# Softmax weights moved into a diagonal matrix product, a shorter pipeline, and another order in the delta-rule scan, in a three-block transformer kernel

## The reference, cut to what matters

```python
# first block: three branches per head, 8 heads of 64, gated and added
p_c = softmax(q @ k_cmp.T + bias)      # 31 compressed keys
p_s = softmax(q @ k_slc.T + bias)      # causal keys, selected blocks
p_w = softmax(q @ k_win.T + bias)      # causal keys, window
out = g0 * (p_c @ v_cmp) + g1 * (p_s @ v_slc) + g2 * (p_w @ v_win)

# third block: 768 keys (256 of context, 512 of the sequence)
o_diff = softmax(q1 @ k1.T) @ v - lam * softmax(q2 @ k2.T) @ v   # 4 heads
o_mla  = softmax(qn @ kn.T + qr @ kr.T) @ v                      # 4 heads

# second block, the gated delta rule, in 8 chunks of 64 tokens, 4 heads
new    = u[chunk] - w[chunk] @ state          # "fresh"
answer = q_dec[chunk] @ state + a_qk[chunk] @ new
state  = g_end * state + k_dec[chunk].T @ new
```

## Time and profile before

| | us |
|---|---|
| median of 3 runs (4128.83 to 4129.73) | 4129.71 |
| the profiled execution | 4129.73 |
| its span in the trace | 4127.9 |
| PE busy | 3511.0 (85%) |
| DVE busy | 2328.0 (56%) |
| ACT busy | 1536.9 (37%) |

### The profile page before, as it was taken

How to read it: one execution, slowest core, us unless ns; L and a number is a source line. 1 busy time by engine, 2 the same in 40 slices (tenths; PEclk the granted TensorE clock), 3 DMA queues, 4 the chain that set the end, 5 groups by cost and what they waited for, 6 DMA issues and landing times. The chain is left out here.

```text
span 4127.9 us, 45959 instructions
## 1 busy us (share of the span) xinstructions
PE 3511.0 (85%) x15671; PEld 2637.0 (64%) x15672; DVE 2328.0 (56%) x2916; ACT 1536.9 (37%) x1926; POOL 140.4 (3%) x124
## 2 busy tenths in 40 slices
PE   6778798999958688899879778775999999999996
PEld 4646687774446457688652645554777777777774
DVE  3355675338232245445440547435888888888885
ACT  1143332010023431110110215314777777777772
POOL 0000000000000100000000000002000000000001
PEclk8889999999979899699989889977999999999997
DMA  4311222222111100022216300116999999999995
GB/s 144 104 47 42 82 91 93 77 95 82 62 36 46 32 11 1 27 95 99 81 61 232 102 31 19 34 58 273 387 361 366 353 362 365 355 350 363 363 351 197
DMA packets 172315, 653.53 MB, mean 158 GB/s; under 512 B 14953, under 2 KB 82377, under 8 KB 114226
## 3 DMA queue, kind: packets, MB, share of 16 engines
q1 hardware_dynamic: 154370, 605.44, 40.2%
q0 software_dynamic: 7568, 25.70, 1.7%
q10 hardware_dynamic: 10272, 20.98, 1.3%
HBM read 610.98 MB, written 36.77 MB: 157 GB/s over the span
## 5 line engine op out<-in xcount | busy, mean ns | idle before, releaser
L378 DVE TENSOR_TENSOR experts_rest<-experts_weights,experts_leading 128x2048 fp32r<-128x2048 f32 x384 | 875.3, 2286 | 100.1 <-ACT experts_leading L2894 100.1
L2894 ACT CAST experts_leading<-experts_weights 128x2048 fp32r<-128x2048 f32 x384 | 715.4, 1904 | 46.9 <-ACT experts_y L2886 23.1
L384 PE MATMUL psum<-experts_leading,experts_xT_leading 128*128 128x512 f32 x1024 | 409.3, 400 | 51.6 <-DVE experts_rest L378 51.6
L385 PE MATMUL psum<-experts_rest,experts_xT_leading 128*128 128x512 f32 x1024 | 406.8, 397 | 0.0
L386 PE MATMUL psum<-experts_leading,experts_xT_rest 128*128 128x512 f32 x1024 | 402.5, 393 | 0.0
L384 PEld LDWEIGHTS psum<-experts_leading,experts_xT_leading 128*128 128x128 f32 x1024 | 194.6, 190 | 107.8 <-DVE experts_rest L378 65.4
L386 PEld LDWEIGHTS psum<-experts_leading,experts_xT_rest 128*128 128x128 f32 x1024 | 194.4, 190 | 44.6
L385 PEld LDWEIGHTS psum<-experts_rest,experts_xT_leading 128*128 128x128 f32 x1024 | 194.9, 190 | 40.2
L384 PE MATMUL psum<-experts_leading,experts_hidden_leading 128*128 128x512 f32 x512 | 210.3, 411 | 0.0
L386 PE MATMUL psum<-experts_leading,experts_hidden_rest 128*128 128x512 f32 x512 | 202.0, 394 | 0.0
L385 PE MATMUL psum<-experts_rest,experts_hidden_leading 128*128 128x512 f32 x512 | 200.9, 392 | 0.0
(11 more groups left out here) (664 smaller groups left out, 6923.2 us busy)
## 6 DMA issues: line engine op xcount, KB each, us to landing
experts_weights<-in_w_up SPq DMA_DIRECT2D x256, 1024.0 KB, 6.9
experts_weights<-in_w_down SPq DMA_DIRECT2D x128, 1024.0 KB, 6.8
merge_weights<-in_w_merge SPq DMA_DIRECT2D x32, 768.0 KB, 4.2
ada_weights<-in_w_ada SPq DMA_DIRECT2D x24, 1024.0 KB, 6.8
ff_up_weights<-in_w_up SPq DMA_DIRECT2D x22, 1024.0 KB, 4.8
expert_rows<-experts_y ACTq DMA_DIRECT2D x66, 256.0 KB, 7.2
down_weights<-in_w_down SPq DMA_DIRECT2D x16, 704.0 KB, 5.1
out_weights<-in_w_out SPq DMA_DIRECT2D x6, 1536.0 KB, 8.7
```

The costliest lines, as they stand in the source:

```text
L378: return dve.tensor_tensor(out, src, leading.bitcast(F32), ALU.subtract)
L384: pe.matmul(out, lh, rh, start=start, stop=False)
L385: pe.matmul(out, lh, rl, start=False, stop=False)
L2894: act.copy(leading[h % LEADING], place(ring, h)).then_inc(masked, 1)
```

## The change

In `paired_attention` the probabilities are no longer scaled. `weigh` writes a diagonal matrix per half (identity times factor, [128 x 2 x 128] in one DVE operation), and `turn` multiplies the raw probabilities with it, as a matrix product instead of a transpose. Where the pair is `joined`, the two halves are added in PSUM, so both are turned. LAG becomes 1 and 2 instead of 2 and 3, with the buffers one less deep, and `weigh(s)` is done in step s (wide) or `weigh(s - 1)` (narrow). In the scan, the state part of the answer moves from before the update to behind it, head by head, paired with the second part.

```diff
-    LAG, HELD = (2, 1) if wide else (3, 2)
+    LAG, HELD = (1, 1) if wide else (2, 2)
...
+        diag = sb("diag", [P, DEEP, 2, P])
...
-                    for h in hs if not joined else (0,):
+                    for h in hs:
                         for n, (lo, keys, _) in enumerate(u.tiles):
-                            last = pe.transpose(k.psum[0:keys, turned_at(h) + n * P:turned_at(h) + (n + 1) * P],
-                                                probs[:, b, h, lo:lo + keys], k.c("ident"))
+                            last = pe.matmul(k.psum[0:keys, turned_at(h) + n * P:turned_at(h) + (n + 1) * P],
+                                             probs[:, b, h, lo:lo + keys], diag[:, b, h, :],
+                                             start=(not joined or (h == 0 and n % (BANK // P) == 0)),
+                                             stop=(not joined or h == 1), skip_group_check=joined)
...
-                    if joined:
-                        dve.tensor_scalar(probs[:, b, 0, 0:u.keys], probs[:, b, 0, 0:u.keys], inverse[:, b, 0:1], None,
-                                          ALU.mult).then_inc(scaled, 1)
-                        dve.wait_ge(scaled, p + 1)
-                        dve.scalar_tensor_tensor(probs[:, b, 0, 0:u.keys], probs[:, b, 1, 0:u.keys], inverse[:, b, 1:2],
-                                                 probs[:, b, 0, 0:u.keys], ALU.mult, ALU.add).then_inc(weighed, 1)
-                    else:
-                        dve.tensor_tensor(probs[:, b, :, 0:u.keys], probs[:, b, :, 0:u.keys],
-                                          inverse[:, b, :].unsqueeze(2).broadcast_to([P, 2, u.keys]), ALU.mult
-                                          ).then_inc(weighed, 1)
+                    if p >= DEEP:
+                        dve.wait_ge(turned, per * (p - DEEP + 1))
+                    dve.tensor_tensor(diag[:, b, :, :], k.c("ident").unsqueeze(1).broadcast_to([P, 2, P]),
+                                      inverse[:, b, :].unsqueeze(2).broadcast_to([P, 2, P]), ALU.mult).then_inc(weighed, 1)
...
-                    v = step - (LAG - 1)
+                    v = step if wide else step - 1
```

In the scan:

```diff
-                    if n >= 2:
-                        pe.wait_ge(taken, n - 1)
-                    answer = k.psum[:, (2 + n % 2) * BANK:(2 + n % 2) * BANK + H * C].rearrange("p (h c) -> p h c", h=H)
-                    for h in range(H):
-                        pe.matmul(answer[:, h, :], state[:, n % 2, h, :], q_dec[:, h, tok], start=(h == 0), stop=False,
-                                  skip_group_check=True)
                     pe.wait_ge(corrected, n + 1)
...
                     last.then_inc(learned, 1)
+                    if n >= 2:
+                        pe.wait_ge(taken, n - 1)
                     for h in range(H):
                         hs = slice(h * P, (h + 1) * P)
-                        last = pe.matmul(answer[:, h, :], fresh[rows, n % 2, hs],
...
+                        o = k.psum[:, (2 + n % 2) * BANK + h * C:(2 + n % 2) * BANK + (h + 1) * C]
+                        pe.matmul(o, state[:, n % 2, h, :], q_dec[:, h, tok], start=True, stop=False)
+                        last = pe.matmul(o, fresh[rows, n % 2, hs], a_qk[rows, t, h * P + rows.start:h * P + rows.stop],
+                                         start=False, stop=True)
                     last.then_inc(answered, 1)
```

More of the change, by code:

```diff
@@ L864, in paired_attention @@
         top, total, inverse = (sb(x, [P, DEEP, 2]) for x in ("top", "total", "inverse"))
+        diag = sb("diag", [P, DEEP, 2, P])
         turned_sb = sb("turned", [P, 2, 2 * BANK])
-        scored, masked, exped, inverted, gated, scaled, weighed, turned, copied, summed, taken, passed = (sem(x) for x in (
-            "scores_ready", "scores_masked", "probs_ready", "sums_inverted", "inverses_gated", "probs_scaled", "weights_ready", "probs_turned",
+        scored, masked, exped, inverted, gated, weighed, turned, copied, summed, taken, passed = (sem(x) for x in (
+            "scores_ready", "scores_masked", "probs_ready", "sums_inverted", "inverses_gated", "weights_ready", "probs_turned",
             "probs_copied", "values_summed", "results_taken", "waits_passed"))
@@ L2125, in _ @@
                     last.then_inc(learned, 1)
+                    if n >= 2:
+                        pe.wait_ge(taken, n - 1)
                     for h in range(H):
                         hs = slice(h * P, (h + 1) * P)
-                        last = pe.matmul(answer[:, h, :], fresh[rows, n % 2, hs],
-                                         a_qk[rows, t, h * P + rows.start:h * P + rows.stop], start=False, stop=(h == H - 1),
-                                         skip_group_check=True)
+                        o = k.psum[:, (2 + n % 2) * BANK + h * C:(2 + n % 2) * BANK + (h + 1) * C]
+                        pe.matmul(o, state[:, n % 2, h, :], q_dec[:, h, tok], start=True, stop=False)
+                        last = pe.matmul(o, fresh[rows, n % 2, hs], a_qk[rows, t, h * P + rows.start:h * P + rows.stop],
+                                         start=False, stop=True)
                     last.then_inc(answered, 1)
```

## The result

| | before | after |
|---|---|---|
| median, us | 4129.72 | 4196.35 (4 runs, 4187.81 to 4198.76) |
| profiled execution, us | 4129.73 | 4197.81 |
| its span | 4127.9 | 4196.0 |
| PE / DVE / ACT busy | 3511.0 / 2328.0 / 1536.9 | 3581.7 / 2292.7 / 1538.5 |

The ratio after to before is 1.0163, 95% interval 1.0150 to 1.0175 (over all 21 executions of the changed kernel, 4187.81 to 4203.06): by the medians 66.6 us slower, where 52.9 were forecast. The time lies inside the range of 4165 to 4200, near its upper end.

What follows compares the result with a forecast made beforehand. PE was taken to bound all four stages, with DVE close in nsa and diff. Terms of 29.7 (diff), 10.5 (nsa), 5.9 (mla) and 6.8 (scan) gave +52.9 on 4129.73: 4182.6 us, range 4165 to 4200.

Steps and rivals of the forecast that it cites:

- The price of a product: Attention turns: 0.23 us per fp32 product, two records of 0.115 as in the fox stretch, against 0.11 to 0.13 per transpose.
- The rivals with cheap products: Attention turns: products cost as little as transposes (0.11; 4136 us; chance 0.04) or about 0.06 (4121 us; chance 0.03).
- the chain rival: diff and nsa: with the short lag the dependency loop binds, not PE; +8 us each, 4199 in all; chance 0.15.
- First turn hidden in the gap, second in the open: mla: first turn grows 0.74 into a wait of 0.94, second adds 0.74 per pair, x 8 = +5.9 us.
- with the low clock until 2484.6: diff: laid out from 2465.1 at the low clock until then, the stage ends at 2570.6 instead of 2540.9, +29.7 us.
- the clock rival: Heads of nsa and diff: denser PE work gets the high clock at once, realistically 8 us less, 4175; chance 0.08.
- the tiles: nsa: longer turns over 160 transposes of 128 keys and 32 of 31 keys add 4.6 us per head pair, 18.5 in all.
- the shorter lag: diff: its loop of 5.69 us stays under PE's 5.83 per pair; mla: 0, bound -2; no separate term in nsa.
- The 8 given back: nsa: of 4.6 us PE waiting per head pair 2.6 remain as DVE scaling shrinks; 2.0 returned each, 8 in all.
- The gap of 0.85: Scan: PE idles 0.85 us per chunk ahead of the update (L2114), waiting for DVE's `fresh`; x 8 = +6.8.
- The same 1.90 of L2118 comes later: Scan: the moved state part keeps its 1.90 us, so the chunk grows by 0.85 only.
- The "relief" of DVE: Less DVE scaling buys back 8 us in nsa and 0.23 x 16 = 3.7 in diff.

Runs made afterwards that it cites:

- The attentions alone: The changed `paired_attention` with the scan as in the kernel before; 4175.35 us, ratio 1.0104 to the kernel before.
- the products with the identity: The kernel before with each transpose replaced by an fp32 product with the identity, scaling and lag as before; 4156.09 us, ratio 1.0056.
- the diagonal with the old lag: The changed attentions with LAG 2 and 3 as before, and the old scan; 4172.51 us, ratio 1.0091 to the kernel before.
- the lag alone: The kernel before with only LAG 1 and 2, transposes and DVE scaling kept; 4171.48 us, ratio 1.0096.
- the blocks: The kernel before with the scan's state part behind the update as one block of four, not head by head; 4140.18 us, one run.
- the copy put first: The kernel before with ACT, in mla only, copying the second half ahead of the next exponential; 4118.90 us, ratio 0.9979.

## Why the prediction was right, and where it wasn't

**The price of a product: right.** 0.116 per record in diff and 0.121 with the identity, 0.115 priced from fox. The products' cost is all of mla and most of diff and nsa. The rivals with cheap products fall.

**The total: right in part by luck.** Measured less forecast, the four stages are off by +7.9 (nsa), +12.1 (scan), -7.2 (diff) and -0.2 (mla). The range reached up to 4200 for the sake of the chain rival, with its 8 us each in diff and nsa; half of that came in nsa, none in diff. What filled the range was mostly the scan's order, which no rival had.

**mla: right, step by step.** First turn hidden in the gap, second in the open, step 10.07 against 10.1.

**diff: the mechanism right, the size 7.2 too large.** The pair takes 5.70 to 5.71 instead of 5.83, PE bound, as said: 16 x 0.13 = 2.1. The other 5.1 is put down to the term "with the low clock until 2484.6", 19.5 into the stage: the full clock now came after 3.4 (1.00 over the attention, before: 0.87). The attentions alone bear this out: the same instructions at the low clock for 7.4 us more took 2.3 longer, which for 16 us makes 5.0, an estimate. That is the clock rival, at some 5 of its 8 us. Why it rose isn't settled. The kernel before and the five variants that leave diff as it was had it after 19.5 to 19.6; the products with the identity after 16, the attentions alone after 10.8, the diagonal with the old lag after 3.1 with a fall between 6.5 and 13.4. But the lag alone, whose turns are all transposes, had it after 9.3, and the attentions alone have the changed kernel's very instructions. The Trainium skill, page "TensorE: Matmul & The Clock Gate", Part 4, has it that transposes don't count as PE activity in the same way. The lag alone shows that this can't be the whole of it, since it rose 10 us earlier with the same transposes. No run here isolates that rule.

**nsa: wrong by 7.9.** Three steps failed. First, the tiles: turns of 4, 8, 12, 16 records take 0.64, 1.09, 1.54, 1.98, some 0.1 more than priced, and 31-key turns 0.55; by these the work grows by 23.4, not 18.5 (by the profile's busy time, from 93.0 to 115.8, by 22.8). I had laid fox's spacing end to end without the group's own edges. Inside a turn records start 0.112 apart, but the first stands up to 0.213 from the second, and the last 0.205 from the values, whose weights have another shape (`128*64` behind `128*128`). In diff, where the values have the turn's shape, that last one is 0.111. Second, "the shorter lag" was priced at nothing in nsa, and is worth 4.5 there. The chain rival had this ("with one step less of slack"), and was right in nsa on the cause, with half its size, though not in diff. Third, the waits given back were laid to DVE's smaller scaling; the two variants between show that this is worth 0.8 beside the longer turns, and that what goes back, goes because PE's longer turns cover the waits (they fall by 7.5 in the identity variant). The 8 given back came out right for the old lag for a wrong reason: PE's waits were 13.7 before, 5.3 with the diagonal and the old lag, 9.3 in the changed kernel. The account closes: 22.8 of work instead of 18.5 (+4.3) and 4.4 given back instead of 8 (+3.6) make 7.9.

**The scan: wrong by 12.1.** The gap of 0.85 is right to the hundredth. The step that failed is "The same 1.90 of L2118 comes later": it comes later and interleaved, and the order of two kinds of product was priced at nothing. Per chunk 0.85 for the gap; ten changes of the weights' shape instead of three, seven more at 0.19, make 1.33; and 0.11 is lost because the update no longer has the second part right behind it (there the next record started 0.107 later, half of the 0.213 inside a block). Together 2.29 for each of seven chunks. The first chunk, which begins at the full clock, grew by 8.79 - 5.91 = 2.88: 18.9 in all, as measured. Of this the blocks show 0.85 + 0.19 + 0.11 = 1.15, the interleaving the other 1.14.

The "relief" of DVE (35 us less to do) gives next to nothing back by itself: 0.8 in nsa, nothing in mla, and in diff the 0.23 of waiting per pair that the longer turns cover too. What it does in diff is to make the short lag bearable. In all four stages PE has the most work, and it took 70.7 more.

## What to carry to other kernels

A change that moves work from a busy engine to the busiest one is priced by the latter's records alone; what the former gains counts only where it still ends a wait after the first has grown. A term that says "the same instructions, only in another order" needs a price of its own on PE: count how often the order changes the shape of the weights, rows or columns. And a wait in the profile is worth most where one instruction in the wrong place on a third engine makes it: the copy put first gave 6.5 us by one instruction moved, where the whole change cost 66.6.

## What the hardware showed that was not expected

- Between fp32 products with weights on 128 rows and on 64 rows each change cost 0.19 us in an interleaved row at the granted clock of 0.50 (1.2 GHz): +1.14 for six. Between two kinds whose weights are both 64x128 it was nothing, and between weights of 128x64 and 128x128 it was 0.19 again. At full clock no experiment measured it; the edges of the turns in nsa there (0.205 and up to 0.213 where 0.112 is the rule) are of that size, 0.09 and 0.10.
- A stage of the same instructions had the full clock at different times: nsa 12.7 to 22.8 us after its start over variants that leave it as it was, and mla fell back to 0.50 for some us in two of them (77.0 and 75.4 long instead of 73.7).
- The short lag cost diff 24.6 us by itself and nothing beside the diagonal products: its loop of 5.90 fell to some 4.9 (an estimate), under PE's 5.70, and what lies under the bound adds nothing.
